# Splitting the weight tiles: the upper parts on ScalarE instead of GpSimd

## The chip, the cores and the metric

The kernel runs on one core of one Trainium2 chip. The metric is the device time of one execution in microseconds (us). Five engines of the core work beside each other, each through its own instructions in order: TensorE (PE in the profile, its weight loads PEld), VectorE (DVE), ScalarE (ACT), GpSimd (POOL) and SyncE (SP), which here only issues DMAs. An engine waits for another by a semaphore.

## The reference

One inference step of a two-layer bidirectional backbone on 128 context tokens and 512 latent tokens (640 together), 1024 channels. For each layer:

```python
h = rms_norm(x, norm_w) * (1 + scale) + shift
proj = h @ w_in                       # 1024 x (2048 + 1024 + 32 + 3*1024 + 2*1024)
y_m = ssd_branch(...)                 # conv of 5 taps, SiLU, chunked scan in both directions, RMSNorm
y_g = gmlp_branch(...)                # gelu, LayerNorm, 128x128 mixing of positions, SiLU gate
merged = sigmoid(gl_m) * (y_m @ w_out_m) + sigmoid(gl_g) * (y_g @ w_out_g)
x = x + gate * (merged @ w_out)
```

and a last RMSNorm. All in float32; the outputs are the two token streams and the final scan states of the context.

## The kernel before

**Tiles.** Each layer multiplies 88 weight tiles of 1024 x 128 (t = 0 to 175 over both layers; p = t mod 88). In a layer p = 0 to 23 are 16 tiles for the convolution and 8 for v (p = 3, 4, 9, 10, 15, 16, 22, 23), 24 to 39 u and z, 40 to 55 alternately the gate glg and the output projection of the gMLP, 56 to 63 z of the scan branch, 64 to 79 the gate glm and its projection, 80 to 87 the output projection.

**Two parts of a number.** TensorE multiplies in the format fp32r. A float32 value is split into a rounded upper part (`hi`) and the rest (`lo`), and every product is made as hi*hi + lo*hi + hi*lo. So a tile is 48 matmuls of 320 columns (60 of 256 for a v tile), in 8 chunks of 128 rows of the weight.

**Weight path.** `w_st`, `w_hi` and `w_lo` have two slots each; tile t uses slot t mod 2. SyncE loads tile t into `w_st` when tile t-2 is fully split (`w_split`). GpSimd then waits for the landing (`w_landed`) and for TensorE to be done with tile t-2 (`tile_done`, line 509), which frees `w_hi` and `w_lo` of the slot. It works in quarters of a tile (2 x 128 columns): `split_hi` (line 513) copies a quarter of `w_st` into `w_hi`, `split_lo` (line 517) subtracts it from `w_st` into `w_lo` and counts `w_split` up. TensorE waits for `w_split` before each chunk: quarter q serves chunks q and q+4, which it takes in the order 0, 4, 1, 5, ... So between the end of tile t-2 and the start of tile t there is the length of tile t-1 in which the first quarter has to be made.

**What ScalarE does.** It evacuates the accumulators of many tiles and applies the functions of the reference, in an order written out by hand: for p < 24 in program order (copy of the raw row at L1184 or, for the first three rows of layer 1, L1093; copies of stands inside the next tile; then `conv_tanh` at L1145, which waits for VectorE's five taps at L1629 and L1631); for 24 to 55 in the order of `order_act`, which sorts items by a place in units of 1/8 of a tile; after that again in program order. The items "b" of `order_act` are the 20 units of the scan output of a layer (L1263 to L1283, with DMAs issued from ScalarE's queue at L1218 and L1227); TensorE's part of unit b stands inside a tile, 6 chunks after that of unit b-1, and needs the masks (L1711) of two units before.

**Start of layer 1.** The first three tiles of layer 1 run on unnormalised rows; ScalarE and VectorE make the norm, h (L1049, L1478, L1484) and the first rows of the convolution (L1093, L1504) while TensorE runs these tiles. TensorE then goes on with two v tiles, p = 3 and 4.

Of the kernel before, what the change touches and what calls it, by code (L numbers as in the profile page):

```python
# [18 lines left out]
P = 128  # L19
DEPTH, DM = 2, 1024  # L20
KC = DM // P
# [119 lines left out]
def order_act():  # L141

    out = [(8 * (T_UZ + n + 1), "uz", n) for n in range(16)] + [(8 * (T_G + 2 * j + 1), "glg", j) for j in range(8)]
    out += [(8 * p + k + 0.5, what, n) for (p, k), what, n in STANDS if p > T_UZ and what in ("a", "b")]
    out += [(8 * 27 + 4, "root", 0)] + [(8 * p + k + 5, "yghi", j) for j, (p, k) in enumerate(SP_AT)]
    return [(what, n) for at, what, n in sorted(out)]
# [35 lines left out]
def build(nc, xT, wts, wada, cT, bada, normw, finalw, ssmw, convw, dtb, alog, dskip, lnw, lnb,  # L182
# [133 lines left out]
    w_split, tile_done, w_go = sem("w_split"), sem("tile_done"), sem("w_go")  # L316
# [74 lines left out]
    def raw_buf(p):  # L391

        return c_buf[2 if p in ("dt", 2) else 3]

# [91 lines left out]
    def _(pool):  # L486
# [14 lines left out]
        def quarter(w, slot, q):  # L501

            return w[:, slot, :].rearrange("p (b q n) -> p q b n", b=2, n=P)[:, q, :, :]

        def split(slot, landed, done):

            pool.wait_ge(w_landed[slot], landed)
            if done is not None:
                pool.wait_ge(tile_done, done)
                pool.sem_inc(w_go, 1)  # L510
# [10 lines left out]
        for slot in range(2):  # L521
            split(slot, 16, None)
            split_hi(slot, 0)
            for q in range(WQ):
                if q + 1 < WQ:
                    split_hi(slot, q + 1)
                split_lo(slot, q, base + WQ * slot + q + 1)
        with pool.Fori(1, DEPTH * NT // 2) as i:
            for slot in range(2):
                split(slot, 16 * i + 16, 2 * i + slot - 1)  # L530
                split_hi(slot, 0)
                for q in range(WQ):
                    if q + 1 < WQ:
                        split_hi(slot, q + 1)
                    split_lo(slot, q, 2 * WQ * i + (base + WQ * slot + q + 1))
# [426 lines left out]
    def _(act):  # L962
# [5 lines left out]

        def pieces(a, dst_ctx, dst_lat, L):
# [72 lines left out]
        for L in range(DEPTH):  # L1042
# [41 lines left out]
            else:  # L1084
# [11 lines left out]
                raw_conv(0)  # L1096
                evacuated(act, ("dt", L))
# [56 lines left out]
            for p in range(T_UZ):  # L1154
# [3 lines left out]
                if p in V_AT:  # L1158
                    j, half = divmod(V_AT.index(p), 2)
                    if half == 1:  # L1160
# [5 lines left out]
                          ACT.Gelu_apprx_tanh).then_inc(v_made, 1)  # L1166
                    if L > 0 and p == RAWT + 1:
                        conv_tanh(NRAW - 1)
# [3 lines left out]
                if L > 0 and i < NRAW:  # L1172
                    if i > 0:
                        raw_conv(p)
                        conv_tanh(i - 1)
# [9 lines left out]
                free(t, last)  # L1185
                if i == (4, 5)[L]:
# [43 lines left out]
            for what, n in order_act():  # L1230
# [8 lines left out]
                elif what == "uz":  # L1239
# [4 lines left out]
                    else:  # L1244
                        if n > 1:
                            evacuated(act, t - 2)
                        A(halves(c_buf[0]), acc_of(t)[:, :, 0:HALF], ACT.Tanh, scale=0.5).then_inc(zt_ready, 1)
                    if n == 12:
# [5 lines left out]
                elif what == "glg":  # L1254
# [3 lines left out]
                    free(t, A(halves(c_buf[0]), acc_of(t)[:, :, 0:HALF], ACT.Tanh, scale=0.5))  # L1258
                else:
# [30 lines left out]
            for j in range(8):  # L1290
# [3 lines left out]
                A(halves(c_buf[0]), acc_of(t)[:, :, 0:HALF], ACT.Tanh, scale=0.5).then_inc(zt_ready, 1)  # L1294
                act.wait_ge(y2_ready, 8 * L + j + 1)
# [9 lines left out]
            for j in range(8):  # L1305
                t = T0 + GLM_AT[j]
                act.wait_ge(tile_done, t + 1)
# [6 lines left out]
                free(t, A(halves(c_buf[j % 2]), acc_of(t)[:, :, 0:HALF], ACT.Tanh, scale=0.5))  # L1314
                if j == 0:
                    root(2 * L + 1)
                    continue
                if j == 1:
                    act.wait_ge(rbc_ready, 2 * L + 2)
                    A(c_buf[2][:, CTX:TOK], X[0][:, :], ACT.Copy, scale=0.5)  # L1320
                    A(c_buf[2][:, 0:CTX], X[1][:, 0:P], ACT.Copy, scale=0.5).then_inc(ry_ready, 1)
                merge_hi(j - 1)
            merge_hi(KC - 1)
            warm_root()
            for j in range(8):
# [18 lines left out]
                evacuated(act, T0 + T_OUT + j)  # L1344
                if j == 7:
# [687 lines left out]
```

## Time and profile before

| | |
|---|---|
| time, median of 3 runs (lowest, highest) | 1440.89 us (1440.36, 1442.1) |
| span of the profiled execution | 1438.0 us |
| PE busy | 1422.0 us, 99% |
| DVE busy | 983.8 us, 68% |
| ACT busy | 474.4 us, 33% |
| POOL busy | 1027.1 us, 71% |
| chain that ended last, by engine | PE 96%, DVE 2% |

The span runs from the first to the last instruction of the profiled execution; the profile gives no other time for it. The median of the runs is 2.9 us above the span, for what lies around it. Busy is the time in which an engine executes; the chain is the series of steps that, followed back from the last instruction, sets the end.

### The profile page before, as it was taken

Reading aid. Unit: us, or ns where it says so; the run is one execution under the profiler, and the core shown is the slowest. Engines: PE = TensorE matmul, PEld = TensorE weight load, DVE = VectorE, ACT = ScalarE, POOL = GpSimd, SP = SyncE. Lnnn points to the kernel's source line nnn. Section 1 sums busy time; section 2 is a strip of 40 time slices with the busy share of each in tenths; the row PEclk is TensorE's granted clock in tenths of the full one; section 3 lists DMA queues with packets and bytes.
Section 4 is the critical chain, followed back from the end, with each engine's and each line's share of the span. In section 5 each row is a group of like instructions: output and inputs, shape, how many; then the busy total and the mean of one; then the engine's idle time right before and its main releaser. Section 6 shows DMA issues by size and latency. Waiting matters only on the chain.

```text
span 1438.0 us, 27064 instructions
## 1 busy us (share of the span) xinstructions
PE 1422.0 (99%) x10191; PEld 1382.6 (96%) x10191; DVE 983.8 (68%) x1454; ACT 474.4 (33%) x1086; POOL 1027.1 (71%) x1421
## 2 busy tenths in 40 slices
PE   8999999999999999999999999999999999999997
PEld 5999998999999999999999999989999999999997
DVE  5865566674777679889978676567566876868234
ACT  4332223313766423101243323241257661320122
POOL 1688875596655489998859897558765556979772
PEclk9999999999999999999999999999999999999999
DMA  9222333123566465444332242411346665453222
GB/s 359 60 64 75 130 108 121 56 70 110 150 189 192 144 262 197 144 164 145 113 133 74 79 128 87 137 60 59 103 127 182 170 189 187 159 188 120 74 74 89
DMA packets 113838, 189.54 MB, mean 132 GB/s; under 512 B 12736, under 2 KB 76352, under 8 KB 112320
## 3 DMA queue, kind: packets, MB, share of 16 engines
q1 hardware_dynamic: 42736, 138.34, 28.8%
q10 hardware_dynamic: 70992, 49.63, 11.7%
q8 instruction: 81, 1.33, 0.4%
q14 instruction: 29, 0.24, 0.0%
HBM read 169.79 MB, written 18.15 MB: 131 GB/s over the span
## 4 chain that ended last, share of the span: by engine, by line
PE 96%; DVE 2%; DMA 0%; ACT 0%; issue 0%; DVEq 0%; SPq 0%; ACTq 0%
PE acc L603 78%; PE acc L570 6%; PE X L843 2%; PE X L808 2%; PE X L570 1%; PE X L828 1%; PE X L875 1%; PE X L854 1%; PE X L762 1%; DVE cv L1631 1%; PE acc L721 0%; DVE ssq L1432 0%; DMA xr<-in_xT 0%; DVE h_pre L1484 0%; DVE xr L1949 0%; PE X L815 0%
## 5 line engine op out<-in xcount | busy, mean ns | idle before, releaser
L513 POOL CAST w_hi<-w_st 128x256 fp32r<-128x256 f32 x704 | 419.3, 609 | 388.7 <-issue 187.3
L517 POOL TENSOR_TENSOR w_lo<-w_st,w_hi 128x256 fp32r<-128x256 f32 x704 | 645.8, 927 | 0.0
L603 PE MATMUL acc<-h_hi,w_hi 128*128 128x320 f32 x1744 | 406.2, 314 | 0.8 <-ACT h_hi L1049 0.8
L603 PE MATMUL acc<-h_lo,w_hi 128*128 128x320 f32 x1744 | 397.8, 309 | 1.5 <-DVE h_lo L1478 1.5
L603 PE MATMUL acc<-h_hi,w_lo 128*128 128x320 f32 x1744 | 397.4, 309 | 0.0
L603 PEld LDWEIGHTS acc<-h_hi,w_hi 128*128 128x128 f32 x1744 | 288.6, 188 | 10.6 <-issue 7.5
L603 PEld LDWEIGHTS acc<-h_lo,w_hi 128*128 128x128 f32 x1744 | 291.5, 188 | 2.2 <-DVE h_lo L1478 2.0
L603 PEld LDWEIGHTS acc<-h_hi,w_lo 128*128 128x128 f32 x1744 | 291.5, 188 | 0.0
L1631 DVE SCALAR_TENSOR_TENSOR cv<-raw,convw_sb,cv 128x642 f32<-128x642 f32 x128 | 134.9, 1054 | 4.5
L1391 DVE SCALAR_TENSOR_TENSOR ada_acc<-ada_st,sc,ada_acc 128x512 f32<-128x512 f32 x112 | 107.1, 995 | 1.8
L1145 ACT ACTIVATE cvt<-cv 128x642 f32<-128x642 f32 x32 | 23.8, 743 | 158.1 <-DVE cv L1631 158.1
L570 PE MATMUL acc<-w_hi,h_hi 128*128 128x256 f32 x256 | 73.2, 286 | 0.0
L570 PE MATMUL acc<-w_hi,h_lo 128*128 128x256 f32 x256 | 72.5, 283 | 0.0
L570 PE MATMUL acc<-w_lo,h_hi 128*128 128x256 f32 x256 | 72.4, 283 | 0.0
L1617 DVE TENSOR_TENSOR xw<-x_tok,ex 128x256 f32<-128x256 f32 x80 | 45.9, 617 | 37.7 <-PE X L808 37.4
L1735 DVE SCALAR_TENSOR_TENSOR gdt<-gm,tm,gdt 128x128 f32<-128x128 f32 x160 | 68.6, 487 | 1.2 <-ACT gdt L1283 0.9
L1629 DVE TENSOR_SCALAR cv<-raw,convw_sb 128x642 f32<-128x642 f32 x32 | 25.9, 811 | 63.4 <-ACT raw L1184 63.3
L1273 ACT ACTIVATE dmat<-cum_bc,ncf 128x128 f32<-128x128 f32 x160 | 62.5, 390 | 12.8 <-issue 11.5
L1314 ACT ACTIVATE c_buf<-acc 128x640 f32<-128x640 f32 x16 | 11.3, 705 | 156.7 <-PE acc L603 156.7
L1275 ACT ACTIVATE cum_bc<-cum_bc,ebs 128x128 f32<-128x128 f32 x160 | 62.0, 388 | 0.0
L603 PE MATMUL acc<-yg_hi,w_hi 128*128 128x320 f32 x256 | 60.2, 316 | 0.0
L1283 ACT ACTIVATE gdt<-gm,tm 128x128 f32<-128x128 f32 x160 | 51.1, 390 | 24.7 <-DVE gm L1746 18.0
(257 smaller groups left out, 2468.4 us busy)
## 6 DMA issues: line engine op xcount, KB each, us to landing
w_st<-in_wts SPq DMA_DIRECT2D x176, 512.0 KB, 3.6
cum_bc<-cum_dram ACTq DMA_DIRECT2D x80, 256.0 KB, 5.0
ada_st<-in_wada SPq DMA_DIRECT2D x33, 512.0 KB, 4.4
ex_bc<-ex_dram ACTq DMA_DIRECT2D x64, 128.0 KB, 3.2
ada_pre<-in_wada SPq DMA_DIRECT2D x15, 512.0 KB, 10.0
mga_dram<-c_buf SPq DMA_DIRECT2D x16, 320.0 KB, 6.0
xf<-xf_dram SPq DMA_DIRECT2D x4, 1280.0 KB, 7.2
mga<-mga_dram SPq DMA_DIRECT2D x2, 2560.0 KB, 9.9
```

Of the source, the lines that this page charges most:

```text
L513: nc.gpsimd.tensor_copy(quarter(w_hi, slot, q), quarter(w_st, slot, q)).then_inc(s_pool, 1)
L517: nc.gpsimd.tensor_tensor(quarter(w_lo, slot, q), quarter(w_st, slot, q), f(quarter(w_hi, slot, q)), ALU.subtract).then_inc(w_split, 1)
L570: last = mm(out.rearrange("p (t n) -> p t n", t=2), x[:, k, P * c:P * (c + 1)], w[:, s, :].rearrange("p (t k n) -> p k t n", t=2, n=P)[:, ...
L603: last = mm(a[:, hf, 0:n1], w[:, s, cols], x[:, k, hf * HALF:hf * HALF + n1], start=(k == 0 and n == 0), stop=(k == KC - 1 and n == 2))
L808: mm(X[3][:, cols], bt[:, s, :], xw[:, s, :, :, :].rearrange("p d h w -> p (d h w)")[:, cols], start=True, stop=True).then_inc(s_mm, 1)
L1273: last = A(dmat[:, n % 2, h, :], cum_bc[n % 2][:, 0, h, :], ACT.Identity, bias=ncf[:, c, j:j + 1])
L1275: last = A(cum_bc[n % 2][:, 1, h, :], cum_bc[n % 2][:, 1, h, :], ACT.Identity, bias=ebs[:, c, j:j + 1])
L1283: last = A(gdt[:, n % 2, h, :], gm[:, n % 2, 1, :], ACT.Copy, scale=tm[:, c, j:j + 1])
L1391: STT(out=o, in0=w, scalar=s, in1=o, op0=ALU.mult, op1=ALU.add)
L1617: last = TT(xw[:, a % 2, d, :, :], xg, per_head(ex[:, d, c, HPG * g:HPG * (g + 1)], HD), ALU.mult)
L1631: ins = STT(out=o, in0=r[:, tap:tap + CW], scalar=w[:, tap:tap + 1], in1=o, op0=ALU.mult, op1=ALU.add)
L1735: last = STT(out=gdt[:, s, h, :], in0=gm[:, s, 0, :], scalar=tm[:, c, j:j + 1], in1=gdt[:, s, h, :], op0=ALU.mult, op1=ALU.add)
```

## The change

The first two tiles are split by GpSimd as before. For all others ScalarE copies the upper parts, in two halves of a tile (128 x 512 each, two quarters), and GpSimd, after each half, makes the two lower quarters. The waits for `w_landed` and `tile_done` move from GpSimd to ScalarE, which counts a new semaphore `whi_ready`; GpSimd waits for that alone.

```diff
+    out += [(8 * (p - 1) + 0.2, "w", p) for p in range(T_G + 3, T_ZM + 2, 2)]      # order_act
...
         with pool.Fori(1, DEPTH * NT // 2) as i:
             for slot in range(2):
-                split(slot, 16 * i + 16, 2 * i + slot - 1)
-                split_hi(slot, 0)
                 for q in range(WQ):
-                    if q + 1 < WQ:
-                        split_hi(slot, q + 1)
-                    split_lo(slot, q, 2 * WQ * i + (base + WQ * slot + q + 1))
+                    if q % 2 == 0:
+                        pool.wait_ge(whi_ready, 4 * i + (2 * slot + q // 2 + 1 - 4))
+                    nc.gpsimd.tensor_tensor(quarter(w_lo, slot, q), quarter(w_st, slot, q), f(quarter(w_hi, slot, q)),
+                                            ALU.subtract).then_inc(w_split, 1)
...
+        def weight_hi(t):                                                          # ScalarE
+            if t >= DEPTH * NT:
+                return
+            s = t % 2
+            act.wait_ge(w_landed[s], 16 * (t // 2 + 1))
+            act.wait_ge(tile_done, t - 1)
+            for q in (0, 2):
+                out, src = (w[:, s, :].rearrange("p (b q n) -> p q b n", b=2, n=P)[:, q:q + 2, :, :] for w in (w_hi, w_st))
+                A(out, src, ACT.Copy).then_inc(whi_ready, 1)
...
                 raw_conv(0)
+                weight_hi(T0 + 2)                       # layer 1, first row
...
+                    weight_hi(t + 2)                    # v tiles: after the gelu, or at once in the first of a pair
                     if L > 0 and p == RAWT + 1:
                         conv_tanh(NRAW - 1)
                     copies(p + 1)
...
                     if i > 0:                           # layer 1, rows 1 and 2 (p = 1, 2)
                         raw_conv(p)
+                        weight_hi(t + 2)
                         conv_tanh(i - 1)
                         (dt_exp, dt_log)[i - 1]()
...
                 free(t, last)                           # other rows of the convolution
+                weight_hi(t + 2)
...
+                    weight_hi(t + 2)                    # after each u and z tile
...
+                    weight_hi(t + 2)                    # after each glg tile
+                elif what == "w":
+                    weight_hi(T0 + n)                   # odd tiles 43 to 57
...
+                weight_hi(t + 2)                        # z of the scan branch, before the square
...
+                if j > 1:
+                    weight_hi(t + 1)
                 act.wait_ge(tile_done, t + 1)           # glm tiles
...
+                weight_hi(t + 2)
...
+                if j == 1:
+                    weight_hi(T0 + T_M + 4)
                 merge_hi(j - 1)
+            weight_hi(T0 + OM_AT[KC - 1] + 2)
...
                 evacuated(act, T0 + T_OUT + j)
+                weight_hi(T0 + T_OUT + j + 2)           # output projection, before part_copy and the square
```

## Rows read from the trace of the kernel before

**Rows 1.** The page: busy time by engine; the last chain's shares by engine.

```profile
PE 1422.0 (99%) x10191; PEld 1382.6 (96%) x10191; DVE 983.8 (68%) x1454; ACT 474.4 (33%) x1086; POOL 1027.1 (71%) x1421
...
PE 96%; DVE 2%; DMA 0%; ACT 0%; issue 0%; DVEq 0%; SPq 0%; ACTq 0%
```

**Rows 2.** The page's costliest groups: count | busy us, mean ns | idle before, releasers.

```profile
L513 POOL CAST w_hi<-w_st 128x256 fp32r<-128x256 f32 x704 | 419.3, 609 | 388.7 <-issue 187.3
L517 POOL TENSOR_TENSOR w_lo<-w_st,w_hi 128x256 fp32r<-128x256 f32 x704 | 645.8, 927 | 0.0
```

**Rows 3.** Who waited for whom, TensorE: us in total, times, longest.

```profile
PE acc L603 <- DVE h_lo L1478: 1.5, 2, 1.0
```

**Rows 4.** Groups of ScalarE's instructions, columns as in rows 2.

```profile
L1263 ACT ACTIVATE dmat<-dmat 128x512 f32<-128x512 f32 x40 | 25.1, 628 | 25.6 <-DVE dmat L1757 23.7 <-issue 1.9
...
L1238 ACT ACTIVATE yg_hi<-c_buf 128x640 fp32r<-128x640 f32 x16 | 11.7, 732 | 0.1
...
L1314 ACT ACTIVATE c_buf<-acc 128x640 f32<-128x640 f32 x16 | 11.3, 705 | 156.7 <-PE acc L603 156.7
```

**Rows 5.** Timeline of GpSimd, 599 to 604 us: start, us, instruction, [idle before].

```profile
599.34 0.73 POOL L517 TENSOR_TENSOR w_lo<-w_st,w_hi 128x256 fp32r<-128x256 f32 x1
...
602.56 1.31 POOL L517 TENSOR_TENSOR w_lo<-w_st,w_hi 128x256 fp32r<-128x256 f32 x1
```

**Rows 6.** Timelines of VectorE, ScalarE and TensorE around tiles 24 and 112.

```profile
190.99 0.68 DVE L1629 TENSOR_SCALAR cv<-raw,convw_sb 128x642 f32<-128x642 f32 x1
...
215.45 1.03 DVE L1629 TENSOR_SCALAR cv<-raw,convw_sb 128x642 f32<-128x642 f32 x1
...
220.56 0.74 ACT L1145 ACTIVATE cvt<-cv 128x642 f32<-128x642 f32 x1 [13.13 <-DVE cv L1631]
...
219.63 0.46 PE L603 MATMUL acc<-h_hi,w_hi 128*128 128x320 f32 x2
...
918.15 0.74 ACT L1145 ACTIVATE cvt<-cv 128x642 f32<-128x642 f32 x1 [13.13 <-DVE cv L1631]
```

**Rows 7.** Timelines of the three engines at the start of layer 1.

```profile
733.66 2.00 DVE L1921 SCALAR_TENSOR_TENSOR p_lo<-xr,amul,p_hi 128x128 fp32r<-128x128 f32 x2 [1.77 <-ACT p_hi L1354]
...
737.00 0.71 PE L754 MATMUL X<-ident,rst 128*128 128x128 f32 x5
...
747.61 3.78 DVE L1478 SCALAR_TENSOR_TENSOR h_lo<-h_pre,mods,h_hi 128x128 fp32r<-128x128 f32 x8
...
752.11 5.90 DVE L1478 SCALAR_TENSOR_TENSOR h_lo<-h_pre,mods,h_hi 128x128 fp32r<-128x128 f32 x8
...
767.31 1.69 ACT L1093 ACTIVATE raw<-c_buf,bsh 128x128 f32<-128x128 f32 x3
...
764.49 0.28 PE L570 MATMUL acc<-w_hi,h_hi 128*128 128x256 f32 x1
```

**Rows 8.** Timelines of ScalarE, VectorE and TensorE in the units b.

```profile
405.70 0.63 ACT L1263 ACTIVATE dmat<-dmat 128x512 f32<-128x512 f32 x1 [2.13 <-DVE dmat L1757]
...
411.61 0.63 ACT L1263 ACTIVATE dmat<-dmat 128x512 f32<-128x512 f32 x1 [1.01 <-DVE dmat L1757]
...
476.34 0.70 ACT L1258 ACTIVATE c_buf<-acc 128x640 f32<-128x640 f32 x1 [2.71 <-issue]
...
450.37 0.69 DVE L1711 TENSOR_TENSOR mmat<-dmat,gdt 128x512 f32<-128x512 f32 x1
...
441.30 1.09 PE L828 MATMUL X<-mmat,x_tok 128*64 128x128 f32 x16
...
455.31 1.09 PE L828 MATMUL X<-mmat,x_tok 128*64 128x128 f32 x16
...
480.60 0.46 PE L603 MATMUL acc<-h_hi,w_hi 128*128 128x320 f32 x2
```

**Rows 9.** Stretches: us, busy of PE, PEld, DVE, ACT, POOL, PEclk, DMA share, GB/s.

```profile
1426.00:1430.00 4.00, 2.34 (x20) 2.08 (x18) 2.84 (x6) 0.97 (x3) 0.00 (x0) 1.00 0.36 131
...
1432.00:1434.00 2.00, 0.00 (x0) 0.00 (x0) 2.00 (x5) 0.00 (x0) 0.00 (x0) 0.51 0.82 291
```

More of the change, by code:

```diff
@@ L315, in build @@
     w_landed = [sem("w_landed0"), sem("w_landed1")]
-    w_split, tile_done, w_go = sem("w_split"), sem("tile_done"), sem("w_go")
+    w_split, tile_done, whi_ready = sem("w_split"), sem("tile_done"), sem("whi_ready")
     acc_free = [sem("acc_free0"), sem("acc_free1")]
@@ L393, in raw_buf, with quarter @@
         return c_buf[2 if p in ("dt", 2) else 3]
+    def quarter(w, slot, q):
+        return w[:, slot, :].rearrange("p (b q n) -> p q b n", b=2, n=P)[:, q, :, :]
     def halves(buf):
@@ L499, in _, with split @@
                                 base=0, pattern=[[-1, P]], channel_multiplier=1).then_inc(consts_made, 1)
[L501 to L510, printed above, removed]
+        def split(slot):
+            pool.wait_ge(w_landed[slot], 16)
         def split_hi(slot, q):
@@ L521, in _ @@
         for slot in range(2):
-            split(slot, 16, None)
+            split(slot)
             split_hi(slot, 0)
```

## The prediction

> **What bounds the kernel now.** I read the page first: TensorE is busy for 1422.0 of 1438.0 us, and it makes up 96% of the chain that ended last [rows 1]. Then the waits of TensorE: the largest wait of a projection matmul on another engine is 1.5 us in total, for VectorE's h_lo; no row has it waiting for GpSimd [rows 3]. Idle time on the whole is 1438.0 - 1422.0 = 16 us, and none of it is put down to the weights. So a faster weight path has nothing to give back. The change can only keep the time or create a wait that isn't there. What has to be read is therefore how late ScalarE reaches each new copy, and I went through the timelines of ScalarE and TensorE side by side for this.
>
> **What is removed and added.** GpSimd has 704 casts with 609 ns on the mean and 704 subtractions with 927 ns [rows 2]; 4 x 174 = 696 of the casts go, 696 x 0.609 = 424 us of its time. All of it lay beside TensorE, so it counts nothing by itself. ScalarE gets 2 x 174 = 348 copies of 128 x 512 from SBUF to SBUF. The trace of before has none; the nearest are the 128 x 512 activation with 628 ns and the 128 x 640 one into fp32r with 732 ns [rows 4]. I take 0.62, with ends 0.60 and 0.73: 1.24 us per tile, 216 us in all, against 964 us in which ScalarE is idle [rows 1].
>
> What a quarter costs on GpSimd depends on VectorE: the same subtraction takes 0.73 us in one place and 1.31 in another [rows 5]. The Trainium skill, "SBUF — State Buffer", section "SBUF: two separate sides", gives VectorE and GpSimd a common port pair that one instruction holds to its end, and ScalarE its own. By that rule the copies on ScalarE never lengthen and VectorE is slowed less. The 1.31 beside the 0.73 agrees with it. It works for the change, and I take its size below from rows 6 and 7 alone.
>
> **How late a tile may be.** Before, GpSimd started a tile the moment TensorE left tile t-2 and had the length of one tile for the first quarter. Now the order is: ScalarE reaches its place in its program, 0.62 for the first half, about 0.1 for the two semaphores, 0.73 to 1.31 for the first subtraction: 1.45 to 2.0 us, call it 1.6. In most places ScalarE is waiting for the very tile that it then evacuates (for example 16 times, 156.7 us of waiting, in the glm stage [rows 4]), so the copy starts some 0.7 us after tile t ends and is ready at 0.7 + 1.6 = 2.3 us, of 7 us or more. That is free. The later subtractions need 0.73 to 1.31 us each while TensorE takes 1.76 us for the two chunks of a quarter, so only the first quarter counts. The load is no later than before, since w_split is complete earlier or at the same time. Three places are different, because there ScalarE is in front of an instruction that waits for VectorE.
>
> *Tile 24 of each layer.* Its copy stands behind conv_tanh of the last convolution row, which ScalarE ends at 220.56 + 0.74 = 221.30, after waiting 13.13 us for VectorE [rows 6]. TensorE starts tile 24 at 219.63 [rows 6]. Ready would be 221.3 + 1.6 = 222.9 (222.75 to 223.3): 3.3 us late. The first instruction of VectorE's row took 1.03 us beside GpSimd's split of this same tile, and 0.68 in an earlier row; as the split isn't running then, 0.35 us come back [rows 6]. 2.9 us, range 2.4 to 3.4. In layer 1 the same wait of 13.13 us ends at 918.15 [rows 6], the same 2.9 us. Together 5.8. What is queued behind the copy on ScalarE (the copies of stands, the gelu of v) moves by 1.24 us, less than TensorE does, so nobody waits for it.
>
> *Tile 4 of layer 1 (t = 92).* Its copy stands behind raw_conv(2). ScalarE ends that at 767.31 + 1.69 = 769.00, TensorE starts the tile at 764.49 [rows 7]: 4.5 us too late before any copy is made, 6.1 us with the 1.6. Two corrections. The copy for t = 89 is put ahead of part_copy, the square and p_hi at the layer's end. VectorE already waits 1.77 us for p_hi and ends p_lo at 735.66; TensorE's broadcast of the norm is at 737.00, 1.34 later [rows 7]. The three short instructions between them (sum, root, reciprocal) I put at 0.7, an estimate, so 0.6 of the 1.24 is hidden and the whole opening comes 0.6 us later. Against that, VectorE sets this stretch: its eight h_lo instructions took 3.78 us in one place and 5.90 in the next, where GpSimd splits [rows 7]. With GpSimd nearly idle until its copy is there, about half of these 2.1 us and some tenths of four later instructions come back: 1.7 us, range 0.8 to 2.5. So 6.1 + 0.6 - 1.7 = 5.0 us, range 3.7 to 6.3. Behind the late copy wait GpSimd, TensorE, and conv_tanh(1) on ScalarE; the last has 3 us of waiting for VectorE to lose. At the next tiles ScalarE has 5 us more than before, as TensorE is that much behind.
>
> *Units b (tiles 40 to 55 of each layer).* This is the only stage in which ScalarE is near full. From one exponential to the next it needs 411.61 - 405.70 = 5.9 us, the issue of four DMAs included [rows 8]. TensorE takes two units in 455.31 - 441.30 = 14.0 us, 7.0 each [rows 8]. A glg evacuation adds 0.70 in 14 us, 0.35 a unit; the copies add 1.24 for each tile, and a unit is 6 chunks of 8: 0.93. Sum 5.9 + 0.35 + 0.93 = 7.2 against 7.0: ScalarE falls back by 0.2 us a unit, 4 us in 20 units. What TensorE has in hand: the mask made at 450.37 to 451.06 is used at 455.31, 4.2 us later [rows 8]. And the copy for tile 54 stands behind the evacuation that ends at 476.34 + 0.70 = 477.04, ready at 478.6 for a start at 480.60, 2.0 us in hand [rows 8]. So the lag and what is in hand are equal. I take 0.5 us a layer, 1.0 together; ends 0 and 4 a layer.
>
> **Sum.** 5.8 + 5.0 + 1.0 = 11.8 us on the span of 1438.0, 1449.8; the median of the runs is 2.9 above the span, so 1440.9 + 11.8 = 1452.7.
>
> **The rivals.**
> - *ScalarE becomes the bound in the units b.* For: 7.2 against 7.0, and its program has waits in it (for gm, for y_out before the DMA issue) that don't all shrink when it is late. Against: at 405.70 and 411.61 it had waited 2.1 and 1.0 us, a part of which is real slack. If another 0.5 us of each unit stays idle, it is 7.7 against 7.0, 14 us in 20 units, less 4 in hand: about 10 a layer at worst, half of that as a middle: 1452.7 + 9 = 1462.
> - *The clock.* Nowhere in the trace does TensorE stand still for 5 us and then go on. At the end its granted clock is 1.00 in 1426 to 1430, where it is busy for 2.34 of 4 us, and 0.51 in 1432 to 1434, where it does nothing [rows 9]; that is the step from 2.4 to 1.2 GHz. If the stall at t = 92 brings it about, the matmuls behind it take double until it is back. Half a tile at half rate costs 3.5 us, a quarter 1.8: 1455 to 1456. The Trainium skill, "TensorE: Matmul & The Clock Gate", section "Part 1: The HAM clock gate (the "warmup" mystery)", says that the gate goes to half rate after idling and back after sustained work, and so speaks for this one; the end of this trace agrees. The stalls at tiles 24, of about 3 us, might do it too.
> - *Not slower.* Its place is the position of the copies at tiles 24 and t = 92. The price of 10.8 us is due only if ScalarE ends conv_tanh and raw_conv(2) after TensorE is there. Both hang on VectorE. If freeing VectorE from the casts brought those ends forward by more than 3.3 and 6.7 us, nothing would be late: at the upper end, VectorE would have to win 6.7 us in the 30 us before 767, where the excess beside GpSimd is 2.1 us in the h_lo instructions [rows 7] and by my estimate 1 more in the rest. Then the time would be 1440 to 1442, and below 1438 only if TensorE's own 16 us of idleness shrank too, for which nothing speaks.
> - *The late tiles cost less than I count,* because a place comes before a wait that I put after it: one of the three falls away, 1446 to 1449.
>
> **How the numbers follow.** Forecast 0.62 (own range 1449 to 1456), ScalarE as the bound 0.13, clock 0.12, one place falls away 0.06, not slower 0.07. A measurement of this kernel can tell about 0.2%, 2.9 us, from no change. Slower by more: 0.62 + 0.13 + 0.12 + 0.06 = 0.93, less a bit for places that I misread: 0.90. Within 0.06, faster 0.04. The range of 8 in 10 leaves out the "not slower" case below and the worst of ScalarE as the bound above: 1448.5 to 1462.
>
> **What would show it.** TensorE's waits list, nearly empty now, would have waits of its matmuls for GpSimd's subtraction: 2.9 us in front of tile 24 of each layer and 5 us at the second v tile of layer 1, one of each, with ScalarE's copy right behind conv_tanh and raw_conv. ScalarE busy about 690 us, its copies 0.60 to 0.65 us each whatever VectorE does; GpSimd near 600 us. The stretch of the units b would be as long as before to within 1 us. I am wrong if these places show no wait, if the units b are longer by more than 2 us, if a copy takes over 0.75 us, or if the granted clock is below 1 inside the span.

## The result and the profile after

The changed kernel takes 1453.19 us (median of 4 runs, 1451.9 to 1454.23), beside 1440.68 us (4 runs, 1440.36 to 1442.1) for the kernel before on the same chip. The ratio is 1.0086, with a 95% interval of 1.0074 to 1.0098: 12.5 us slower. The forecast was 1452.7, range 1448.5 to 1462.

The profiled execution took 1453.56 us with a span of 1451.5, against 1438.0 before. First the page of the changed kernel: busy time by engine, the engines' shares of the last chain, and two of its costliest groups.

```profile
PE 1428.1 (98%) x10191; PEld 1386.0 (95%) x10191; DVE 970.8 (67%) x1454; ACT 650.2 (45%) x1434; POOL 664.8 (46%) x725
...
PE 91%; issue 3%; DVE 3%; ACT 2%; POOL 1%; DMA 1%; SPq 0%; ACTq 0%; DVEq 0%; POOLq 0%
...
L531 POOL TENSOR_TENSOR w_lo<-w_st,w_hi 128x256 fp32r<-128x256 f32 x696 | 654.1, 971 | 736.9 <-ACT w_hi L975 736.9
...
L975 ACT ACTIVATE w_hi<-w_st 128x512 fp32r<-128x512 f32 x348 | 200.1, 627 | 178.3 <-PE acc L600 99.5
```

The work moved as the diff says: against [rows 1], ScalarE went from 474.4 to 650.2 us, GpSimd from 1027.1 to 664.8. The 348 copies last 0.627 us each. TensorE does the same 10191 matmuls, yet is busy for 6.1 us more. Work that stays the same and takes longer is the first hint that waits are not the whole answer.

ScalarE and GpSimd did not come out where the prediction had them, at 690 and near 600 us. Part of it is that two copies of 0.63 us behind each other take 1.13 together, and that GpSimd's subtraction takes 971 ns on the mean where it took 927 [rows 2].

The chain now leaves TensorE in 9% of the span instead of 4%. The waits list says where (who waited for whom: us in total, times, longest), where [rows 3] had only VectorE's h_lo:

```profile
PE acc L600 <- POOL w_lo L531: 3.9, 2, 2.0
PE acc L567 <- POOL w_lo L531: 3.3, 1, 3.3
...
PE acc L600 <- DVE c_buf L1816: 0.6, 2, 0.3
```

Three waits for the weights: two of 2.0 us and one of 3.3, 7.2 us together. The timelines show them in place, tile 24 of layer 0 and then t = 92 (TensorE's first matmul, ScalarE's tanh and copy, GpSimd's subtraction; start, us, instruction, [idle before]):

```profile
219.31 0.74 ACT L1154 ACTIVATE cvt<-cv 128x642 f32<-128x642 f32 x1 [11.42 <-DVE cv L1655]
219.96 1.13 ACT L975 ACTIVATE w_hi<-w_st 128x512 fp32r<-128x512 f32 x2
...
220.65 5.67 POOL L531 TENSOR_TENSOR w_lo<-w_st,w_hi 128x256 fp32r<-128x256 f32 x8 [10.78 <-ACT w_hi L975]
...
221.64 0.53 PE L600 MATMUL acc<-h_hi,w_hi 128*128 128x320 f32 x2 [1.95 <-POOL w_lo L531]
...
769.34 1.54 ACT L1101 ACTIVATE raw<-c_buf,bsh 128x128 f32<-128x128 f32 x3
770.68 1.14 ACT L975 ACTIVATE w_hi<-w_st 128x512 fp32r<-128x512 f32 x2
...
771.38 3.97 POOL L531 TENSOR_TENSOR w_lo<-w_st,w_hi 128x256 fp32r<-128x256 f32 x4 [8.60 <-ACT w_hi L975]
...
772.16 0.39 PE L567 MATMUL acc<-w_hi,h_hi 128*128 128x256 f32 x1 [3.31 <-POOL w_lo L531]
```

Read each from the top: ScalarE waits for VectorE, does its own instruction, and the copy stands right behind it; GpSimd has waited for that copy; TensorE has waited for GpSimd. From the end of the tanh, 220.05, to the first matmul, 221.64, it is 1.6 us.

But 7.2 us of waits are not 13.5 us of span. I compared the end of every tile in the two traces. Tile 24 ends 3.31 us later than before relative to tile 23, t = 92 5.05 us, tile 112 (tile 24 of layer 1) 3.32. Each time more is lost than was waited: 1.36, 1.74 and 1.36 us. The stretches show by what (columns as in [rows 9]; the eighth number is the granted clock):

```profile
221.00:223.00 2.00, 1.36 (x9) 1.39 (x10) 0.00 (x0) 2.00 (x6) 2.00 (x4) 1.00 0.00 0
223.00:225.00 2.00, 2.00 (x7) 1.33 (x6) 0.00 (x0) 0.75 (x2) 2.00 (x4) 0.53 0.10 16
225.00:227.00 2.00, 2.00 (x9) 1.52 (x8) 1.15 (x2) 0.60 (x1) 1.32 (x2) 0.62 0.64 246
227.00:229.00 2.00, 2.00 (x17) 2.00 (x16) 0.00 (x0) 1.04 (x3) 0.00 (x0) 1.00 0.70 143
...
772.00:774.00 2.00, 1.84 (x10) 1.84 (x11) 1.97 (x3) 0.00 (x0) 2.00 (x3) 0.66 0.00 0
774.00:776.00 2.00, 2.00 (x12) 2.00 (x10) 1.97 (x4) 1.88 (x2) 1.35 (x2) 0.50 0.04 8
776.00:778.00 2.00, 2.00 (x18) 2.00 (x18) 1.72 (x3) 1.97 (x5) 0.91 (x2) 0.98 0.69 217
...
931.00:933.00 2.00, 2.00 (x5) 0.85 (x5) 0.00 (x0) 0.01 (x1) 2.00 (x4) 0.50 0.57 145
```

Shortly after TensorE is back at work its granted clock goes from 1.00 to 0.50, that is from 2.4 to 1.2 GHz, for some 3.4 us, behind all three waits. TensorE is "busy" all the while, 2.00 of 2 us, but shows 5 to 12 matmul records in 2 us instead of 17 or 18. So the account of the 13.54 us by which the last tile ends later is:

| place | wait | clock | in all |
|---|---|---|---|
| tile 24, layer 0 | 1.95 | 1.36 | 3.31 |
| t = 92 | 3.31 | 1.74 | 5.05 |
| tile 24, layer 1 | 1.96 | 1.36 | 3.32 |
| tiles 41 | | | 2 x 0.57 |
| small ones between tiles 24 and 41 (0.23 of them at tile 28) | | | 2 x 0.40 |
| start of the kernel and rest | | | -0.08 |

### The profile page after: what moved, and what is told of

Its sections match the earlier page's. It is cut to its first block, busy times and chain, and to the rows that moved or that the text cites. A ratio compares the mean times of both kernels' runs of the same rounds, so it can differ in the third digit from the quotient of the medians.

```text
span 1451.5 us, 26087 instructions
## 1 busy us (share of the span) xinstructions
PE 1428.1 (98%) x10191; PEld 1386.0 (95%) x10191; DVE 970.8 (67%) x1454; ACT 650.2 (45%) x1434; POOL 664.8 (46%) x725
## 3 DMA queue, kind: packets, MB, share of 16 engines
q10 hardware_dynamic: 70992, 49.63, 11.8%
## 4 chain that ended last, share of the span: by engine, by line
PE 91%; issue 3%; DVE 3%; ACT 2%; POOL 1%; DMA 1%; SPq 0%; ACTq 0%; DVEq 0%; POOLq 0%
PE acc L600 75%; PE acc L567 4%; PE X L840 2%; PE X L805 2%; PE X L825 1%; PE X L872 1%; PE X L567 1%; POOL w_lo L531 1%; DMA ada_pre<-in_wada 1%; DVE h_pre L1508 1%; PE X L851 1%; DVE cv L1655 1%; ACT h_hi L1057 1%; PE X L759 1%; PE acc L718 0%
## 5 line engine op out<-in xcount | busy, mean ns | idle before, releaser
L531 POOL TENSOR_TENSOR w_lo<-w_st,w_hi 128x256 fp32r<-128x256 f32 x696 | 654.1, 971 | 736.9 <-ACT w_hi L975 736.9
L975 ACT ACTIVATE w_hi<-w_st 128x512 fp32r<-128x512 f32 x348 | 200.1, 627 | 178.3 <-PE acc L600 99.5
L1655 DVE SCALAR_TENSOR_TENSOR cv<-raw,convw_sb,cv 128x642 f32<-128x642 f32 x128 | 147.1, 1149 | 4.5
L1415 DVE SCALAR_TENSOR_TENSOR ada_acc<-ada_st,sc,ada_acc 128x512 f32<-128x512 f32 x112 | 100.0, 933 | 1.8
L567 PE MATMUL acc<-w_hi,h_hi 128*128 128x256 f32 x256 | 73.9, 289 | 3.3 <-POOL w_lo L531 3.3
L567 PE MATMUL acc<-w_hi,h_lo 128*128 128x256 f32 x256 | 73.0, 285 | 0.0
L567 PE MATMUL acc<-w_lo,h_hi 128*128 128x256 f32 x256 | 73.0, 285 | 0.0
L1735 DVE TENSOR_TENSOR mmat<-dmat,gdt 128x512 f32<-128x512 f32 x40 | 34.6, 864 | 41.2 <-issue 32.9
L1653 DVE TENSOR_SCALAR cv<-raw,convw_sb 128x642 f32<-128x642 f32 x32 | 21.7, 679 | 58.8 <-ACT raw L1195 58.7
L600 PE MATMUL acc<-ym_hi,w_hi 128*128 128x320 f32 x256 | 58.9, 311 | 0.0
L600 PE MATMUL acc<-yg_lo,w_hi 128*128 128x320 f32 x256 | 58.3, 309 | 0.0
```

Of the source, the lines that this page charges most:

```text
L531: nc.gpsimd.tensor_tensor(quarter(w_lo, slot, q), quarter(w_st, slot, q), f(quarter(w_hi, slot, q)), ALU.subtract).then_inc(w_split, 1)
L567: last = mm(out.rearrange("p (t n) -> p t n", t=2), x[:, k, P * c:P * (c + 1)], w[:, s, :].rearrange("p (t k n) -> p k t n", t=2, n=P)[:, ...
L600: last = mm(a[:, hf, 0:n1], w[:, s, cols], x[:, k, hf * HALF:hf * HALF + n1], start=(k == 0 and n == 0), stop=(k == KC - 1 and n == 2))
L975: A(out, src, ACT.Copy).then_inc(whi_ready, 1)
L1415: STT(out=o, in0=w, scalar=s, in1=o, op0=ALU.mult, op1=ALU.add)
L1655: ins = STT(out=o, in0=r[:, tap:tap + CW], scalar=w[:, tap:tap + 1], in1=o, op0=ALU.mult, op1=ALU.add)
```

## The experiments

Theory A: the copies are late at three places because of where they stand in ScalarE's order, and each place costs its wait and a stretch at the lower clock. Rival B: the clock falls for a reason of its own, so only the waits belong to the places. Rival C: what costs is the new weight path or ScalarE's load as a whole.

### The copy of tile 24 ahead of the wait

```
-                    weight_hi(t + 2)
+                    if p != 22:
+                        weight_hi(t + 2)
...
                 copies(p + 1)
+                if i == NCONV - 1:
+                    weight_hi(T0 + 24)
                 conv_tanh(i)
```

> The changed kernel, with the copy of tile 24 of each layer put ahead of the wait of the last conv_tanh instead of behind it; all else as changed. Theory A (the loss arises at three places where a copy stands behind an instruction that waits for VectorE, and each place costs its wait plus a stretch at the lower clock): the 3.3 us at tile 24 of both layers go whole, 6.6 us, wait and clock together: 1446.6 us, 1.0040 of the kernel before; the granted clock stays at 1.00 there; the 5.05 us at the second v tile of layer 1 stay. Rival B (the clock falls for another reason than the wait, so only the two waits of 1.95 us come back): 1449.3. Rival C (what costs is the load on ScalarE or the new weight path as a whole, and the three places only show it): the time stays above 1451.

Measured: 1447.18 us, ratio 1.0047 (1.0031 to 1.0064). Only one wait for the weights is left in the list, `PE acc L567 <- POOL w_lo L531: 3.3, 1, 3.3`, and tile 24 ends even 0.16 us earlier, relative to tile 23, than before. The copy now runs while ScalarE would have waited for VectorE anyway; the timeline of ScalarE:

```profile
211.94 1.16 ACT L975 ACTIVATE w_hi<-w_st 128x512 fp32r<-128x512 f32 x2 [4.17 <-PE X L567]
220.19 0.74 ACT L1154 ACTIVATE cvt<-cv 128x642 f32<-128x642 f32 x1 [7.10 <-DVE cv L1658]
```

Wait and clock went together. Rival C falls by the time; rival B's 1449.3 lies just inside the interval (up to 1.0064, 1449.7 us), and it is the profile that speaks against it: nothing is lost at either tile 24, and the clock stays at 1.00 there. One more thing stands in these two rows. The tanh starts at 220.19, against 219.31 when the copy came late. GpSimd works on tile 24 beside VectorE's last row again, and VectorE is slower for it by 0.9 us. So in the changed kernel the late copy itself shortened the wait that it stood behind.

### The copies of tiles 4 to 11 of layer 1 one place earlier

```
-                    weight_hi(t + 2)
+                    if L > 0 and p in (3, 4, 9):
+                        if p == 4:
+                            weight_hi(t + 3)
+                    elif True:
+                        weight_hi(t + 2)
...
                         raw_conv(p)
-                        weight_hi(t + 2)
+                        weight_hi(t + (2 if p == 1 else 4))
+                        if p == 1:
+                            weight_hi(t + 3)
                         conv_tanh(i - 1)
+                        if p == 1:
+                            weight_hi(t + 4)
...
-                weight_hi(t + 2)
+                weight_hi(t + (3 if L > 0 and p < 9 else 2))
```

> The changed kernel, with the copies of tiles 4 to 11 of layer 1 made one place earlier (the copy of the second v tile ahead of conv_tanh(0), the next ones each one tile ahead); the two tiles 24 as changed. Theory A: the 3.3 us of waiting and the 1.7 us at the lower clock both go at this place: 1448.2 us, 1.0052 of the kernel before. What I am unsure of is whether conv_tanh and raw_conv, now 1.2 us later in ScalarE's order, make VectorE's rows late: then up to 1 us stays. Rival B: 3.3 us come back, 1449.9. Rival C: no change from 1453.

Measured: 1447.44 us, ratio 1.0053 (1.0036 to 1.0069), and no wait at t = 92: its end is 0.00 us later relative to the tile before it. My worry about VectorE's rows came to 0.06 us in all up to tile 98. The time is 0.8 below theory A's 1448.2, and the tile ends say why: tile 24 of layer 0 still cost 3.31 us, the one of layer 1 only 1.69, with the same wait of 1.96 us before it. Rival B's 1449.9 is again inside the interval of the times (up to 1.0069), and again the profile decides: with the wait at t = 92 gone, the clock doesn't fall there. The second wait at a tile 24, and the stretches behind both, in this kernel:

```profile
923.60 0.53 PE L600 MATMUL acc<-h_hi,w_hi 128*128 128x320 f32 x2 [1.96 <-POOL w_lo L531]
...
224.00:226.00 2.00, 2.00 (x5) 0.86 (x4) 0.12 (x1) 0.19 (x1) 2.00 (x4) 0.50 0.64 172
...
924.00:926.00 2.00, 2.00 (x13) 1.76 (x13) 0.00 (x0) 1.71 (x4) 2.00 (x4) 1.00 0.00 0
```

The second wait left the clock alone in this execution. Theory A in its plain form, every such wait brings the fall, is thus wrong in one point, which the last experiments take up.

### TensorE kept busy through the waits

```
+            if t == NT + 4:
+                for _ in range(7):
+                    mm(X[0][:, 0:2 * P], ident[:, :], tri[:, :, :].rearrange("p d n -> p (d n)"),
+                       start=True, stop=True)
...
             acc_ready(t)
+            if t % NT == 24:
+                for _ in range(4):
+                    mm(acc_of(t)[:, 1, 0:2 * P], ident[:, :], tri[:, :, :].rearrange("p d n -> p (d n)"),
+                       start=True, stop=True)
```

> The changed kernel, with idle matmuls whose result nobody reads put on TensorE ahead of the three late tiles: 4 of 128x256 in fp32 before tile 24 of each layer, 7 before the second v tile of layer 1, about 0.43 us each, so that TensorE works through most of the 1.95 and 3.3 us. The copies come as late as in the changed kernel, so the tiles start no earlier. Theory A: the granted clock stays near 1.00 behind the three places and the matmuls keep 0.28 us, which gives back 1.4 + 1.4 + 1.7 = 4.5 us: 1448.7 us, 1.0055. Rival B (the clock falls for another reason): 1453, and the clock of these stretches is still 0.5 to 0.6. A third way: the idle matmuls last longer than the gap and delay the tile by up to 0.4 us each.

Measured: 1448.82 us, ratio 1.0056 (1.004 to 1.0073), against 1.0086 for the changed kernel: 4.4 us less, by matmuls that compute nothing. The timeline of TensorE at both kinds of place, and the clock behind them (the stretches are those in which the changed kernel had 0.53 and 0.50):

```profile
220.41 1.89 PE L586 MATMUL acc<-tri,ident 128*128 128x256 f32 x8
222.43 0.56 PE L608 MATMUL acc<-h_hi,w_hi 128*128 128x320 f32 x2
...
767.90 3.18 PE L559 MATMUL X<-tri,ident 128*128 128x256 f32 x14
771.39 0.39 PE L571 MATMUL acc<-w_hi,h_hi 128*128 128x256 f32 x1 [0.31 <-POOL w_lo L531]
...
223.00:225.00 2.00, 2.00 (x12) 1.63 (x12) 0.00 (x0) 1.63 (x4) 2.00 (x4) 1.00 0.04 8
...
774.00:776.00 2.00, 2.00 (x19) 2.00 (x18) 1.73 (x4) 1.97 (x4) 0.60 (x1) 1.00 0.23 18
```

The three places now cost 1.62, 3.60 and 1.62 us: about the bare lateness. The fall of the clock is a consequence of TensorE standing still, and it was a third of the loss. The Trainium skill, "TensorE: Matmul & The Clock Gate", section "Part 1: The HAM clock gate (the "warmup" mystery)", gives the idle array 1.2 GHz and the busy one 2.4; this run agrees in kind.

This profile also has a fall that the changed kernel's has not, long before the first late tile, where the two programs are the same. The clock in this profile, and then in that of the kernel before:

```profile
36.00:39.00 3.00, 2.37 (x48) 1.93 (x48) 2.92 (x8) 1.19 (x4) 3.00 (x6) 1.00 0.03 8
39.00:42.00 3.00, 2.96 (x10) 2.62 (x11) 3.00 (x6) 2.97 (x8) 0.53 (x1) 0.51 0.35 105
...
39.00:42.00 3.00, 2.42 (x14) 2.14 (x15) 3.00 (x6) 2.97 (x8) 0.54 (x1) 1.00 0.44 94
```

TensorE's waits ahead of 39 us are short and alike in both, 0.98 or 0.99, 0.72 and 0.54 us. Here a fall follows, and TensorE comes out of it some 0.8 us behind the kernel before; there none follows. So whether such a fall comes is not fixed by the program alone. The other three executions of this kernel took 1448.6 to 1449.0 us at a mean granted clock of 0.998, the profiled one 1449.6 at 0.997.

### The kernel before with the waits alone

```
-        with pool.Fori(1, DEPTH * NT // 2) as i:
-            for slot in range(2):
...
+        def pair(i, waits=()):
+            for slot in range(2):
+                if slot == 0:
+                    for s, n in waits:
+                        pool.wait_ge(s, n)
...
+        for n, s, v in ((12, cvt_ready, 16), (46, raw_ready, 3), (56, cvt_ready, 32)):
+            with pool.Fori(at, n) as i:
+                pair(i)
+            pair(n, [(s, v)])
```

> The kernel before, in which GpSimd makes both parts of every tile and ScalarE copies nothing; added are three waits on GpSimd alone: before it splits tile 24 of each layer it waits for the last conv_tanh, and before the second v tile of layer 1 for raw_conv(2). Theory A: the same losses as in the changed kernel to within 0.5 us each, with the same fall of the clock behind them: 1440.7 + 3.3 + 3.3 + 5 = 1452.3 us, 1.0081; less its own layer shift of 0.6 and the 0.57 at tile 41, which belong to the copies and should be missing, and with the h_lo row of VectorE slow as in the kernel before, which delays raw_conv(2) by up to 1.5 us more. So 1451.5 to 1453.5. Rival C (the copies themselves or ScalarE's load cost): 1441 to 1444, since no copy is here.

Measured: 1456.26 us, ratio 1.0106 (1.0089 to 1.0123). No copy is on ScalarE, and it is slower than the changed kernel. Rival C is out; the place costs. The list and the timeline of GpSimd show by how much it is more:

```profile
PE acc L582 <- POOL w_lo L517: 5.5, 1, 5.5
PE acc L615 <- POOL w_lo L517: 5.3, 2, 2.7
...
221.24 1.26 POOL L513 CAST w_hi<-w_st 128x256 fp32r<-128x256 f32 x2 [10.73 <-ACT cvt L1157]
222.47 0.72 POOL L517 TENSOR_TENSOR w_lo<-w_st,w_hi 128x256 fp32r<-128x256 f32 x1
...
772.12 1.56 POOL L513 CAST w_hi<-w_st 128x256 fp32r<-128x256 f32 x2 [10.74 <-ACT raw L1105]
773.65 1.30 POOL L517 TENSOR_TENSOR w_lo<-w_st,w_hi 128x256 fp32r<-128x256 f32 x1
```

The waits are 2.7 and 5.5 us and the places cost 3.96, 7.89 and 3.99: 0.7 and 2.2 more of waiting, because GpSimd casts two quarters (1.26 and 1.56 us) ahead of its first subtraction where ScalarE had the first half ready in some 0.6, and because the opening of layer 1 is as slow as before. The clock part is 1.3 at tiles 24 and 2.4 behind the 5.5, where the clock falls before the wait is over and stays down for some 6.8 us. The fall at 39 us is in this profile too, so some 0.9 of its 16.7 us belong to no late tile. The small losses of the changed kernel (tiles 28 and 41) are all missing, as expected: those do belong to the copies. I had expected the waits of this kernel to be near those of the changed one, with up to 1.5 us more at t = 92, and was 2.8 us too low at the upper end.

### All places mended by order alone

Both moves from above, and:

```
-                    weight_hi(t + 2)
+                    if n < 15:
+                        weight_hi(t + 2)
...
                         last.then_inc(t_ready, 1)
+                        if n == 1:
+                            weight_hi(T0 + 41)
                         act.wait_ge(gm_ready, NU * L + n + 1)
...
-                weight_hi(T0 + T_OUT + j + 2)
+                if j < 7:
+                    weight_hi(T0 + T_OUT + j + 2)
...
                     last.then_inc(phi_ready, 1)
+                    if j == 7:
+                        weight_hi(T0 + T_OUT + j + 2)
```

> The changed kernel with every place mended by order alone, no work taken away: both moves of the two runs before (the copy of tile 24 of each layer ahead of the last conv_tanh, the copies of tiles 4 to 11 of layer 1 one place earlier), and two small ones: the copy of tile 41 inside unit b1, between its masks and its gdt, instead of ahead of the unit, and the copy of tile 1 of layer 1 behind p_hi instead of ahead of it. Theory A: all three stalls go with their clock, and the 0.57 at tiles 41 of both layers and up to 0.6 of the layer's opening; what stays is 0.23 behind tile 28 of each layer, less the 0.37 that tile 24 ended earlier: 1440.4 to 1441.3 us, no difference from the kernel before; VectorE's relief shows in its rows but not in the time, since no other place of before had TensorE waiting for VectorE for more than 1.5 us. Rival C (ScalarE's load costs something everywhere): 1443 or more.

Measured: 1440.77 us (11 runs), ratio 1.0004 (0.9995 to 1.0013). The same number of copies, the same subtractions, and no difference in the time. Span 1438.3, and TensorE is as busy as in [rows 1] again:

```profile
PE 1421.9 (99%) x10191; PEld 1381.8 (96%) x10191; DVE 971.9 (68%) x1454; ACT 651.1 (45%) x1434; POOL 670.9 (47%) x725
```

TensorE's 1421.9 beside the 1428.1 of the changed kernel is the clock given back; ScalarE and GpSimd are as busy as there. The tiles 41 lost nothing here. This is the best version of the change, and it doesn't beat the kernel before: 356 us less on GpSimd and 12 less on VectorE bought nothing, since TensorE's end is set by neither.

### Three tiles of 174 undone, and four

```
+WHOLE = (24, NT + 4, NT + 24)
...
-            if t >= DEPTH * NT:
+            if t >= DEPTH * NT or t in WHOLE:
                 return
```

and GpSimd casts the tiles of WHOLE itself, as the kernel before does.

> The changed kernel, undone for three of its 174 tiles: tiles 24 of each layer and the second v tile of layer 1 (t = 92) are again split whole by GpSimd, without a copy on ScalarE. Theory A: no stall at tiles 24 (6.6 us back) and none at t = 92. But t = 92 was late enough to cover t = 93, whose copy ScalarE reaches only behind conv_tanh(1) and dt_log: in the kernel before dt_log ends at 774.87 us, with the copy and the first subtraction 1.4 to 1.6 more, 776.3 to 776.5, while TensorE wants tile 93 at 771.87. So the stall comes back one tile later with 4.4 to 4.6 us of waiting and a stretch at the lower clock of 1.7 to 2.4: about 6 to 7 us. Sum 1440.4 + 1.7 (the small ones) + 6.5 = 1448.6. Rival: ScalarE gains with the copy that it doesn't make, and t = 93 is at most 1 us late: 1443. Rival C: the loss is in the weight path as a whole, and three tiles of 174 give back next to nothing: above 1451.

Measured: 1445.95 us, ratio 1.0041 (1.0026 to 1.0057), below theory A's 1448.6 and above the rival's 1443. In the profile nothing is lost at t = 24, 92 and 112, and the wait reappears at tile 93, as expected, but as `PE acc L623 <- POOL w_lo L531: 2.1, 1, 2.1` instead of 4.5. ScalarE's timeline there:

```profile
771.04 0.75 ACT L1177 ACTIVATE cvt<-cv 128x642 f32<-128x642 f32 x1 [2.74 <-DVE cv L1678]
...
773.34 1.13 ACT L998 ACTIVATE w_hi<-w_st 128x512 fp32r<-128x512 f32 x2
```

The tanh is at 771.04 instead of 772.46 in the kernel before, although TensorE is 0.9 us later here: VectorE is 2.3 us ahead of what I had taken over from the old trace. It is the same mistake as in the prediction (below). And this wait of 2.13 us left the clock at 1.00 in the profiled execution, so tile 93 lost only 2.37. That execution is the fastest of four, 1444.24 us at a mean granted clock of 0.998. The others took 1445.75 and 1446.14 (both 0.997) and 1447.63 (0.994): the same program lost up to 3.4 us more, at a lower clock. Where it fell in those, no profile shows.

With t = 93 undone too (WHOLE with NT + 5):

> As the one before, with t = 93 split whole by GpSimd too: 4 tiles of 174 are undone. Theory A: then no stall of over 1 us is left. The copies of tiles 94 to 98 come 1.1 to 1.5 us before TensorE wants them and need 1.4 to 1.6, so some tenths each may stay. 1440.4 + 1.7 + 0.5 = 1442.6 us, 1.0015 of the kernel before. Rival C: above 1450.

Measured: 1442.29 us (10 runs), ratio 1.0014 (1.0005 to 1.0023). Four tiles out of 174 hold 10 to 11 of the 12.5 us (1.0086 less 1.0014, or 1453.2 less 1442.3). What is left, 2.1 us, is tiles 28 and 41 and what lies beside them, 0.9 to 1.0 us in each layer.

### How long a wait the clock forgives

In the kernel before, GpSimd repeats the first cast of chosen tiles:

```
+STALLS = ((31, 6), (41, 9), (75, 8), (83, 8))
...
+                    for _ in range(again):
+                        split_hi(slot, 0)
```

> The kernel before, in which GpSimd repeats the first cast of four tiles (t = 62, 82, 150, 166) 6, 9, 8 and 8 times ahead of splitting them, each on the one before, some 0.7 us a time, so that TensorE waits there for about 1.1, 1.9, 2.3 and 0.7 us by my estimate from when GpSimd ends the first quarter in the kernel before. It is to show behind how long a gap the granted clock falls and what that costs. Theory A: behind 1.9 and 2.3 it falls to about 0.5 for some 3 us, as behind the 1.95 us at tile 24 of the changed kernel, and costs 1.3 to 1.7 us beyond the wait; behind 0.7 and 1.1 I have no row, and expect no fall. Rival B (the fall comes from something else at those places): the clock stays at 1.00 at all four and each costs its wait alone.

> The kernel before with ten made gaps on TensorE, as in the run with four of them: GpSimd repeats the first cast of tiles 18, 26, 38, 54, 106, 114, 126, 142, 154 and 172 12 to 16 times, so that by my estimate TensorE waits there for 1.3 to 3.0 us. So far the clock fell behind gaps of 1.95 (twice), 2.52 and 3.31 us, and did not behind 2.0, 2.1 and 2.16. Theory A2 (what decides near 2 us is something that I don't control, and longer gaps all bring it): the gaps of 1.8 to 2.2 fall in part, those of 2.4 and more all fall, those under 1.5 don't; each fall costs 1.3 to 1.6 us beside the wait. Theory A3 (it is the place in the program): gaps at the start of a tile of the same kind behave alike.

> The same kernel as the run before, once more. Theory A2: the gaps last as long to within 0.1 us, but of those near 2 us other ones have the fall behind them than in the first run. Theory A3: the same ones fall in both.

Measured, one execution each: 1447.36 us for the kernel with four repeats (the kernel before 1440.16), 1449.56 and 1449.47 for the one with ten (1440.93). My estimates of the waits were poor: the first kernel gave 2.52 us at t = 62 and 2.16 at t = 150 and next to nothing at the other two; the second gave six between 0.68 and 1.77 us, all shorter than I wanted, the same in both runs to within 0.15. Behind 2.52 the clock fell; behind 2.16, and behind the longest of the second kernel, 1.77 (which the profile puts down to no engine), it did not. The second kernel has no fall in either run, so it could not separate theories A2 and A3:

```profile
544.88 0.53 PE L619 MATMUL acc<-h_hi,w_hi 128*128 128x320 f32 x2 [2.52 <-POOL w_lo L518]
546.00:548.00 2.00, 2.00 (x10) 1.96 (x10) 1.96 (x3) 0.91 (x2) 2.00 (x3) 0.53 0.00 0
...
1246.62 0.53 PE L619 MATMUL acc<-h_hi,w_hi 128*128 128x320 f32 x2 [2.16 <-POOL w_lo L518]
1248.00:1250.00 2.00, 2.00 (x16) 1.91 (x14) 1.99 (x2) 1.32 (x2) 2.00 (x3) 1.00 0.03 8
```

```profile
1277.73 0.53 PE L619 MATMUL acc<-ym_hi,w_hi 128*128 128x320 f32 x2 [1.77 <-issue]
1278.00:1280.00 2.00, 2.00 (x16) 2.00 (x16) 0.00 (x0) 0.00 (x0) 2.00 (x4) 1.00 0.00 0
```

To see whether the cases near 2 us are chance, the changed kernel and the kernel with the early t = 92 ran once more:

> The changed kernel as it is, once more. Theory A2: the waits of 1.95, 1.95 and 3.31 us come out alike, but behind the two of 1.95 the clock may stay at 1.00, each worth 1.4 us of the time, so 1450.4 to 1453.5 us; behind 3.31 it falls. Theory A3: the clock falls behind all three, 1452.5 to 1453.5.

> The kernel with the copies of tiles 4 to 11 of layer 1 made early, once more. In its first run the wait of 1.96 us at tile 24 of layer 0 had the lower clock behind it and the wait of 1.96 us at tile 24 of layer 1 had not; in both profiles of the changed kernel both had. If it is the program and its place in time that decides, the first falls and the second doesn't, again (tile ends later by 3.3 and 1.7 us, 1447 to 1447.5 us in all). If it is chance from execution to execution, another pattern is as likely: both (1449) or none (1446).

In both the falls came where they had come before. The changed kernel, 1453.58 us: falls behind all three (3.32, 5.05, 3.30 us lost). The other, 1447.08 us: a fall behind the 1.95 us at 221.6 us of the span, none behind the 1.96 at 923.6 (3.32 and 1.70 us lost). The same tile, with the same wait, had the fall in the changed kernel, where it comes at 928.6. So it is neither the kind of tile nor the length alone. Chance from execution to execution is not excluded by two pairs of profiles: within each pair the waits ended at the same moments of the span to 0.1 us, the fall at 39 us comes in some profiles and not in others of a program that is the same up to there, and the three whole tiles gave 1444.24 to 1447.63 us at clocks of 0.998 to 0.994. That the moment of the wait within the execution decides is a rival that fits all this and that no run tested.

## Why the prediction was right, and where its terms were not

The sum was 11.8 us and the measured loss 12.5 on the medians, 13.5 on the profiled spans. The three places with large waits were right. The terms were mis-sized, in both directions, and nearly cancelled: that the total comes within 0.7 us is luck. One of the prediction's own signs of being wrong came true, a granted clock below 1 inside the span.

- **The bound, and that a faster weight path has nothing to give.** Right. The mended version has GpSimd and VectorE unloaded and no copy late, and is level with the kernel before (1.0004).
- **The price of a copy.** 0.62 taken, 0.627 measured. From ScalarE's end of the instruction ahead to TensorE's start: 1.6 taken, 1.6 measured at tile 24, and 1.3 at t = 92 (770.88 to 772.16).
- **Tiles 24: 2.9 us each, of which the wait is all.** The step that failed is "0.35 us come back". The tanh ended at 220.05 instead of 221.30 us: 1.25 came back, of which 0.1 is TensorE's lead since the start of the kernel. I counted only the first instruction of VectorE's row against [rows 6]. In fact the instructions ahead of it, the first and the four behind it all got shorter. VectorE, first in the kernel before and then in the changed one:

```profile
214.40 1.13 DVE L1617 TENSOR_TENSOR xw<-x_tok,ex 128x256 f32<-128x256 f32 x2 [6.42 <-PE X L808]
215.45 1.03 DVE L1629 TENSOR_SCALAR cv<-raw,convw_sb 128x642 f32<-128x642 f32 x1
216.51 4.01 DVE L1631 SCALAR_TENSOR_TENSOR cv<-raw,convw_sb,cv 128x642 f32<-128x642 f32 x4
```

```profile
214.30 0.76 DVE L1641 TENSOR_TENSOR xw<-x_tok,ex 128x256 f32<-128x256 f32 x2 [6.42 <-PE X L805]
214.97 0.61 DVE L1653 TENSOR_SCALAR cv<-raw,convw_sb 128x642 f32<-128x642 f32 x1
215.62 3.66 DVE L1655 SCALAR_TENSOR_TENSOR cv<-raw,convw_sb,cv 128x642 f32<-128x642 f32 x4
```

  So the wait was 1.95, below my range of 2.4 to 3.4, and the place cost 3.3 because 1.36 of clock came on top, which the sum did not have.
- **t = 92: 5.0 us.** 5.05 measured, as 3.31 of wait and 1.74 of clock. Two parts of my sum were off. The "0.6 us later" of the opening was 0: p_lo starts 1.0 us later than the tiles around it and takes 1.54 instead of 2.00, so it ends only 0.6 later, at 740.43, and TensorE's broadcast of the norm starts at 741.18, 4.18 after the 737.00 of [rows 7], when the tiles before it are 4.2 late. The slack, which the sum had right at 0.6, was enough, and taking the copy away from there in the mended version changed nothing. And VectorE's relief was larger than 1.7: raw_conv(2) ended at 770.88, 2.3 us earlier than 769.00 plus the 4.2 by which everything was late. The second group of eight h_lo took 3.78 us, not 5.90, and the rows behind gave the rest.
- **Units b: 0.5 us a layer.** Nothing was lost there. Two units take 14.01 us of TensorE as before (the row below and its like at 459.48), so ScalarE as the bound was a false alarm.

```profile
445.47 1.09 PE L825 MATMUL X<-mmat,x_tok 128*64 128x128 f32 x16
```

  The size, 1.0 for the two layers, is by luck near what tiles 41 cost (1.14), which has another reason: the copy of tile 41 stands ahead of unit b1, VectorE's dmat and behind it the evacuation of tile 39 come late, and TensorE waits 0.3 us for the accumulator. I had not seen this place, nor the 0.8 us of small losses between tiles 24 and 41, whose cause stays open.
- **The clock, given 0.12 as a rival.** It was not a rival but a part of what happened, behind 2 us as well as behind 3.3, and worth 4.46 us of the 13.54. I had put it aside at tiles 24 with "might", and priced it at 3.5 or 1.8 at t = 92 alone, where it was 1.74 (with 1.8 the rival's time is 1454.5 us, not the 1455 that I wrote).
- **What I got wrong twice:** that the durations of VectorE in the old trace hold when GpSimd's work beside them changes. It made the waits too long in the prediction and the wait at tile 93 too long in the expectation of the three whole tiles.

So the middle of the forecast was reached with a wait term of 10.8 where 7.2 was measured and a clock term of 0 where 4.5 was.

## What to carry to other kernels

When a step moves to another engine, its price is in most places nothing and in a few places everything: look for the instructions of the new engine that wait for a third one, and put the step ahead of them, not behind. Price a new stall of the bounding engine as the wait plus what its clock loses afterwards, and where the stalled chain shares a resource with what has stopped, expect part of the wait to come back by itself. Where TensorE must wait for 2 or 3 us, some matmuls that nobody reads are worth having there (4.4 us for three such waits here).

## What the runs showed of the hardware

- A wait of TensorE of 1.95 us between two stretches of full work can be followed by some 3.4 us at 1.2 GHz, which cost 1.36 us beside the wait; one of 3.31 cost 1.74, one of 5.50 cost 2.4. With TensorE kept busy through the same time, the granted clock stayed at 1.00.
- Not every such wait does it. In the profiles there is a fall behind waits of 1.95, 1.96 (several profiles), 2.52, 2.66, 3.31 and 5.50 us, and none behind 1.77, 1.96, 2.13 and 2.16. At 39 us, where the longest wait is under 1 us, two profiles have a fall and the others have none. Two kernels profiled twice showed the same falls both times, but the clocks of the executions without a profile differ within one kernel. What decides beside the length stays open.
- The same VectorE instruction on 128x642 in fp32 took 0.61 us with GpSimd at rest and 1.03 beside its cast and subtraction; ScalarE's 128x512 copies took 0.61 to 0.68, 0.627 on the mean, in the changed kernel. The Trainium skill, "SBUF — State Buffer", section "SBUF: two separate sides", has VectorE and GpSimd on a shared port pair and ScalarE on its own; the rows agree. What I had not expected is how far this reaches: freeing VectorE moved the end of one row forward by 1.25 us and of a chain of rows by 2.3.
